# The last attention taken by pairs of heads, with four buffers and query tiles further ahead, and the shared keys and values prepared inside the fifth FFN

## The chip, the cores and the metric

The kernel runs on one core of a Trainium2 chip. The metric is the device time of one execution in microseconds. A profile of one execution shows what each engine did: PE (TensorE, with its weight loads as PEld), DVE (VectorE), ACT (ScalarE), POOL (GpSimd) and SP, which issues the weight transfers.

## What is computed

The reference is two blocks of two layers each on 256 tokens of width 1024, in float32. The first block has a convolution module, a sparse attention and two FFNs. The second puts 16 meta tokens ahead (272 positions) and has four FFNs, a gated linear attention, and last a sliding-window attention with sinks over keys and values that all its layers share. That last attention is what the change is about:

```python
def swa_mixer(hn, w_q, sinks, w_out, k, v, cos, sin):
    q = (hn @ w_q).reshape(B, L, N_KV_HEADS, GROUP, HEAD_DIM)      # 16 heads of 64, 4 to a key head
    q = apply_partial_rope(q, cos, sin) * (HEAD_DIM ** -0.5)
    ...
    # each block of 128 queries sees 16 meta keys, the block before and its own (masked)
    s = jnp.einsum('bkgnqd,bknsd->bkgnqs', q_blk, k_band)
    p = sink_softmax(s, mask, sink)          # exp(s-m) / (sum + exp(sink-m))
    o = jnp.einsum('bkgnqs,bknsd->bkgnqd', p, v_band)
    return o @ w_out
```

The keys and values come from `shared_kv`, a product of the stream after the fourth FFN with `w_kv`, with the keys rotated. They are thus known one FFN before the attention needs them.

## The kernel before

Activations lie transposed, 128 channels on the partitions and the tokens along the free axis, in eight tiles (KD = 8). Every weight tile of 128x1024 float32 comes by DMA into a ring of six slots; ACT makes its high part `wh` (L1704), DVE the low part `wl` (L1828, called through `ahead`), five tiles ahead of its use. A product is then three matmuls for each of eight k-steps (L1584): high by high, low by high, high by low, 24 for a tile of 256 columns.

The order of work on each engine is written out by hand; engines wait on counted semaphores. For unit u = 8 (the last attention) PE runs `swa_pe`, ACT `swa_act`, DVE `swa_dve`. PE first runs `begin`, an opening: it multiplies the first tiles by the high part of x as this arrives, then makes the mean of squares (L1635), from which ACT and DVE make the scale `rx` (L1766, L1845), then adds the low part (L1626). The opening takes two query tiles before; the third follows by itself.

A query tile holds two heads, h = 0 on partitions 0 to 63, h = 1 on 64 to 127. Its rotation is a matmul with `rot` on PE (`perm`, L1336) and three DVE operations (L1445 to L1447: sines, cosines, sum). The 16 heads are units n. For each, PE makes `scores(n)` (L1350, two matmuls of 144 and 272 columns over 64 rows), DVE adds the mask and finds the least (L1476), ACT makes the exponentials with their sums (L1418, L1420), DVE scales by the reciprocal (L1489 to L1492), PE turns the probabilities (`turned`: three large transposes L1361, two of the 16 meta keys L1363), ACT and DVE copy them out (L1429, L1506), PE multiplies by the values (`values`: L1376, L1377, L1379), and ACT and DVE split the result in high and low parts (`attn_hi` L810, `attn_lo` L814). Every one of these buffers is double. PE's loop over n has one query tile's matmuls on even n and one rotation on odd n, tile n // 2 + 3.

The keys' rotation (L1323 and L1445 to L1447) and the turning of the values (L1328, L1330, copies L1405, L1406) stand at the head of this unit. The fifth FFN (`ffn4_a`: 44 tiles, then `ffn4_b`) lies between the product that makes keys and values and this unit.

The earlier sparse attention (unit 2) already runs by pairs: `scores(p)` at L658 alternates two heads in different halves of the rows and different banks, `values(p)` at L695 and L697 two heads in different halves of the output columns, with buffers four deep.

## Time and profile before

| | |
|---|---|
| runs before | 1915.03 us median of 3 (1914.94 to 1917.54) |
| the profiled execution | 1917.76 us, its span 1916.0 us |
| mean granted TensorE clock | 0.957 of full speed |
| PE busy | 1839.4 us, 96% of the span |
| DVE busy | 1247.2 us, 65% |
| ACT busy | 917.1 us, 48% |

PE is busy nearly always by its record, but this is no limit in itself: matmuls are pipelined, and their records double when the granted clock is half. What a change is worth is read from its stretch of the trace: which engine the others wait for there, and at which clock PE ran.

### The profile page before, as it was taken

The numbers are of one execution on the slowest core, as the hardware profiler recorded it, in microseconds if no ns is written. First come the engines' busy times: TensorE is split into PE (matmuls) and PEld (weight loads), VectorE is DVE, ScalarE is ACT, GpSimd is POOL, SyncE is SP. The second block draws the span as 40 slices with busy tenths as digits, with TensorE's granted clock in tenths as the row PEclk, the third lists the DMA queues.
The fourth block names the chain that finished last, engine by engine and source line by source line (L and its number), as shares of the span: only waits on it lengthen the run. The fifth ranks groups of instructions, "written<-read, shape, count | busy, mean of one in ns | idle before, by whom it ended". The sixth has DMA issues, their size and how long they took to land.

```text
span 1916.0 us, 33032 instructions
## 1 busy us (share of the span) xinstructions
PE 1839.4 (96%) x13492; PEld 1711.9 (89%) x13492; DVE 1247.2 (65%) x2120; ACT 917.1 (48%) x1585; POOL 113.3 (6%) x150
## 2 busy tenths in 40 slices
PE   6989998999899999999999999999999998999997
PEld 6979997888479998999979879999999997589997
DVE  6867668774777666766564338665676657557764
ACT  7545443542755454544454235444554545445442
POOL 1001004300010001000100020000000000000000
PEclk9999999997899999999998979999999999789999
DMA  4214555541025555555533214555455551025553
GB/s 153 78 44 165 187 185 202 187 144 45 1 89 185 184 193 193 182 176 176 190 108 101 76 66 144 172 174 191 138 190 185 195 188 62 27 89 200 186 198 122
DMA packets 76038, 276.35 MB, mean 144 GB/s; under 512 B 8496, under 2 KB 9520, under 8 KB 75760
## 3 DMA queue, kind: packets, MB, share of 16 engines
q1 hardware_dynamic: 75168, 270.57, 42.1%
q8 instruction: 107, 1.75, 0.4%
q0 software_dynamic: 288, 2.30, 0.3%
q10 hardware_dynamic: 432, 1.38, 0.2%
q14 instruction: 43, 0.35, 0.1%
HBM read 273.16 MB, written 1.05 MB: 143 GB/s over the span
## 4 chain that ended last, share of the span: by engine, by line
PE 88%; DVE 7%; ACT 3%; DMA 1%; issue 1%; DVEq 0%; SPq 0%; ACTq 0%
PE acc L1584 43%; PE mix L1584 19%; PE acc L1580 4%; PE mix L265 3%; PE acc L1581 2%; PE acc L1604 2%; DVE wl L1828 2%; DMA arrived<-in_w 1%; PE acc L1089 1%; PE acc L1350 1%; PE stat L1635 1%; PE acc L1658 1%; PE acc L1092 1%; PE mix L1658 1%; PE mix L1604 1%
## 5 line engine op out<-in xcount | busy, mean ns | idle before, releaser
L1828 DVE TENSOR_TENSOR wl<-arrived,wh 128x1024 fp32r<-128x1024 f32 x514 | 641.6, 1249 | 400.1 <-ACT wh L1704 388.3
L1704 ACT ACTIVATE wh<-arrived 128x1024 fp32r<-128x1024 f32 x514 | 542.0, 1058 | 585.1 <-DMA arrived<-in_w 584.7
L1584 PE MATMUL acc<-xh,wh 128*128 128x256 f32 (+1 forms) x1512 | 432.6, 286 | 0.0
L1584 PE MATMUL acc<-xh,wl 128*128 128x256 f32 (+1 forms) x1512 | 430.4, 285 | 0.0
L1584 PE MATMUL acc<-xl,wh 128*128 128x256 f32 (+1 forms) x1512 | 430.2, 285 | 0.0
L1584 PE MATMUL acc<-hx,wh 128*128 128x256 f32 (+1 forms) x1664 | 304.3, 284 | 0.0
L1584 PEld LDWEIGHTS acc<-xh,wh 128*128 128x128 f32 x1512 | 287.1, 190 | 5.9 <-issue 5.2
L1584 PEld LDWEIGHTS acc<-xh,wl 128*128 128x128 f32 x1512 | 287.2, 190 | 0.0
L1584 PEld LDWEIGHTS acc<-xl,wh 128*128 128x128 f32 x1512 | 286.1, 189 | 0.2
L1584 PE MATMUL mix<-xh,wh 128*128 128x256 f32 (+1 forms) x968 | 278.8, 288 | 2.3 <-DVE y L1447 1.4
L1584 PE MATMUL mix<-xh,wl 128*128 128x256 f32 (+1 forms) x968 | 277.1, 286 | 0.0
L1584 PE MATMUL mix<-xl,wh 128*128 128x256 f32 (+1 forms) x968 | 276.7, 286 | 0.0
L1584 PEld LDWEIGHTS acc<-hx,wh 128*128 128x128 f32 x1664 | 258.9, 189 | 0.8 <-issue 0.8
L1584 PE MATMUL acc<-hx,wl 128*128 128x256 f32 (+1 forms) x832 | 236.6, 284 | 0.0
L1584 PEld LDWEIGHTS mix<-xh,wh 128*128 128x128 f32 x968 | 185.0, 191 | 5.0 <-DVE y L1447 1.9
L1584 PEld LDWEIGHTS mix<-xh,wl 128*128 128x128 f32 x968 | 185.0, 191 | 0.0
L1584 PEld LDWEIGHTS mix<-xl,wh 128*128 128x128 f32 x968 | 184.4, 191 | 0.2
L1584 PEld LDWEIGHTS acc<-hx,wl 128*128 128x128 f32 x832 | 157.0, 189 | 0.0
L1580 PE MATMUL acc<-hx,wh 128*128 128x512 f32 x416 | 149.1, 401 | 7.8 <-DVE wl L1828 6.8
L1581 PE MATMUL acc<-hx,wl 128*128 128x256 f32 x416 | 117.7, 283 | 0.0
L1580 PEld LDWEIGHTS acc<-hx,wh 128*128 128x128 f32 x416 | 79.3, 191 | 27.8 <-DVE wl L1828 8.0
L1546 POOL TENSOR_TENSOR sumsq<-sq 128x256 f32<-128x256 f32 (+1 forms) x11 | 11.8, 1076 | 1162.7 <-ACT sq L1779 777.0
(408 smaller groups left out, 2339.7 us busy)
## 6 DMA issues: line engine op xcount, KB each, us to landing
arrived<-in_w SPq DMA_DIRECT2D x514, 512.0 KB, 3.3
scr<-in_cmp_w POOLq DMA_DIRECT2D x1, 2048.0 KB, 8.9
x<-in_x ACTq DMA_DIRECT2D x2, 544.0 KB, 8.1
out<-x SPq DMA_DIRECT2D x8, 128.0 KB, 1.8
par<-in_par ACTq DMA_DIRECT2D x1, 259.0 KB, 4.5
scr<-in_positions POOLq DMA_DIRECT2D x1, 128.0 KB, 7.1
scr<-in_cmp_w POOLq DMA_DIRECT2D x1, 32.0 KB, 9.2
scr<-in_w_gate POOLq DMA_DIRECT2D x1, 32.0 KB, 2.9
```

The source lines that it names most:

```text
L265: ins = nc.tensor.matmul(mix[1 + j % 2][:, 0:SEQ], cdiag[:, j % 2, n, :], cu[:, j - 1, s:s + SEQ], start=(n == 0), stop=(n == PE_TAPS - 1))
L1089: ins = nc.tensor.matmul(dst, gv[base:base + w, n, 256 * h + P * v:256 * h + P * v + P], gatt[base:base + w, c % 2, h, 0:w], start=True, s ...
L1092: ins = nc.tensor.matmul(dst, gS[(c - 1) % 2][h][:, P * v:P * v + P], gq[:, h, s:s + w], start=False, stop=True)
L1350: ins = nc.tensor.matmul(acc[n % 2][:, c:c + e], sq_q[DH * h:DH * h + DH, j, q:q + P], sk[DH * h:DH * h + DH, j // 4, 0:e], start=True, st ...
L1580: nc.tensor.matmul(bank(name, t)[:, 0:2 * SEQ], wh[:, h.slot, w], hx[:, :, k, META:], start=(k == 0), stop=False)
L1581: ins = nc.tensor.matmul(bank(name, t)[:, 0:SEQ], wl[:, h.slot, w], hh[:, k, META:], start=False, stop=(k == kt - 1))
L1584: ins = nc.tensor.matmul(bank(name, t)[:, 0:L - c], w_part[:, h.slot, w], v_part[:, k, c:], start=(k == 0 and w_part is wh and v_part is h ...
L1604: nc.tensor.matmul(bank(name, t)[:, 0:L - c], w_part[:, slot, k * P:(k + 1) * P], hi[:, k, c:], start=(k == 0 and w_part is wh), stop=False)
L1635: ins = nc.tensor.matmul(stat[:, 0:L - c], ones[:], sq[:, k, c:], start=(k == 0), stop=(k == KD - 1))
L1658: ins = nc.tensor.matmul(bank(name, t)[:, 0:L - c], w_part[:, slot, w], v_part[:, k, c:], start=(k == 0 and w_part is wh and v_part is xh) ...
L1704: nc.scalar.activation(wh[:, h.slot, :], raw(h.slot), ACT.Copy).then_inc(w_hi, 1)
L1828: nc.vector.tensor_tensor(wl[:, h.slot, :], raw(h.slot), wh[:, h.slot, :].bitcast(F32), ALU.subtract).then_inc(w_lo, 1)
```

## The change

1. The keys' rotation and the turning of the values move into `ffn4_a`: after its tiles 0 to 3, 4 to 11, 12 to 19 and 20 to 27 PE runs one piece of `kv_turned` each, ACT copies after two of its double tiles (`kv_values`), DVE rotates after two (`kv_keys`). All use the bank `stat`. The second head's 16 meta values go to partitions 32 to 47, by an ordinary matmul with the identity and not a transpose.
2. The opening takes four query tiles instead of two, and the loop's query tile is p + 4.
3. The loop goes over eight pairs p of heads. Scores of a pair alternate heads (rows 0 to 63 and 64 to 127, banks `acc[0]` and `acc[1]`), values alternate heads in the halves of the output columns. Scores run two pairs ahead.
4. `sS`, `sP` and `sPT` have four buffers instead of two.
5. DVE scales a pair's probabilities with two tensor_tensor instead of four tensor_scalar, adds and inverts the sums of two heads at once, and copies the small transposes of a pair in one operation on 48 partitions.
6. The sines' part of a rotation is taken apart from the rest (`sines`, `rotated`), with its own semaphore; `attn_lo` runs two pairs behind.
7. ACT reads its exponential table ahead of the unit's first weight split.

```diff
-        sS = area(832).rearrange("p (b n) -> p b n", b=2)
-        sP = area(832).rearrange("p (b n) -> p b n", b=2)
-        sPT = area(768).rearrange("p (b n) -> p b n", b=2)
+        sS = area(1664).rearrange("p (b n) -> p b n", b=4)
+        sP = area(1664).rearrange("p (b n) -> p b n", b=4)
+        sPT = area(1536).rearrange("p (b n) -> p b n", b=4)
...
         def swa_pe(pe, gemm, begin, opening):
-            begin(8, ("swa_q", 0), ("swa_q", 1))
-            pe.wait_ge(s_kv, 4)
-            for m in range(2):
-                ins = nc.tensor.matmul(mix[1 + m][:, 0:L], rot[:], sk[:, m, :], start=True, stop=True)
-                ins.then_inc(s_perm, 1)
...
+            begin(8, ("swa_q", 0), ("swa_q", 1), ("swa_q", 2), ("swa_q", 3))
...
+            def scores(p):
+
+                pe.wait_ge(s_k, p + 1)
+                if p:
+                    pe.wait_ge(s_min, 2 * p)
+                for qt, (c, e, q) in enumerate(SQ):
+                    for h in range(2):
+                        ins = nc.tensor.matmul(acc[h][:, c:c + e], sq_q[DH * h:DH * h + DH, p, q:q + P], sk[DH * h:DH * h + DH, p // 4, 0:e],
+                                               start=True, stop=True)
+                        if qt:
+                            ins.then_inc(s_s, 1)
...
+            def values(p):
+
+                if p >= 2:
+                    pe.wait_ge(m_lo, 24 + p - 1)
+                for part in range(3):
+                    for h in range(2):
+                        n, g = 2 * p + h, 2 * (p // 4) + h
+                        w = slice(DH * g, DH * g + DH)
+                        dst = mix[p % 2][DH * h:DH * h + DH]
+                        if part == 0:
+                            pe.wait_ge(s_ptc, n + 1)
+                            nc.tensor.matmul(dst[:, 0:SEQ], sv[:, 0, w], sPT[:, n % 4, 0:SEQ], start=True, stop=False)
+                        elif part == 1:
+                            nc.tensor.matmul(dst[:, P:SEQ], sv[:, 1, w], sPT[:, n % 4, SEQ:SEQ + P], start=False, stop=False)
+                        else:
+                            pe.wait_ge(s_pmc, p + 1)
+                            r = slice(32 * h, 32 * h + META)
+                            nc.tensor.matmul(dst[:, 0:SEQ], sv[r, 2, w], sPM[r, p % 2, :], start=False, stop=True).then_inc(s_o, 1)
...
+            for p in range(KD + 1):
+                if p:
+                    values(p - 1)
+                if p + 2 < KD:
+                    scores(p + 2)
+                if p + 3 < KD:
+                    perm(p + 3)
+                if p < KD:
+                    turned(p)
+                if p + 4 < KD:
+                    pe.wait_ge(s_turn, p + 4)
+                    gemm("swa_q", xh, xl, META, None, first=p + 4, last=p + 5)
             gemm("swa_out", hh, hl, META, (m_lo, 24))
...
+            for p in range(KD):
+                t = p + 3
+                if 3 < t < KD:
                     query(t)
-                elif t < KD:
-                    rotated(2 + t, sq_q[:, t, :], SEQ, SEQ + META)
...
+                normal(p)
+                if t < KD:
+                    sines(t)
+                if p + 2 < KD:
+                    least(2 * p + 4)
+                    least(2 * p + 5)
+                if t < KD:
+                    rotated(t)
+                if p >= 2:
+                    attn_lo(dve, p - 2, 3)
+                dve.wait_ge(s_pm, p + 1)
+                if p >= 2:
+                    dve.wait_ge(s_o, 2 * p - 2)
+                nc.vector.tensor_copy(sPM[0:32 + META, p % 2, :], stat[0:32 + META, 0:SEQ]).then_inc(s_pmc, 1)
+                if t < KD:
                     ahead(BASE["swa_q"] + t)
...
-                    gemm("ffn4_a", xh, xl, cg(u), (x_lo, 8 * u))
+                    gemm("ffn4_a", xh, xl, cg(u), (x_lo, 8 * u), last=4)
+                    for i in range(4):
+                        kv_turned(pe, i)
+                        gemm("ffn4_a", xh, xl, cg(u), None, first=4 + 8 * i, last=12 + 8 * i)
+                    gemm("ffn4_a", xh, xl, cg(u), None, first=36)
```

On PE, what lay between two query tiles of the loop before (L1361 and L1363 turn one head, L1350 its scores, L1376 to L1379 its values, L1336 a rotation):

```order
L1361 MATMUL acc<-ident,scr 128x128 x3
L1363 MATMUL stat<-ident,scr 16x128 x2
L1350 MATMUL acc<-scr,y 128x144
L1350 MATMUL acc<-scr,y 128x272
L1376 MATMUL mix<-scr 64x256
L1377 MATMUL mix<-scr 64x128
L1379 MATMUL mix<-scr 64x256
L1336 MATMUL mix<-y,rot 128x256
L1361 MATMUL acc<-ident,scr 128x128 x3
L1363 MATMUL stat<-ident,scr 16x128 x2
```

and what lies there after the change (L1415 to L1421 values, L1379 scores, L1370 rotation, L1391 to L1401 the turning of a pair):

```order
L1415 MATMUL mix<-scr 64x256 x2
L1417 MATMUL mix<-scr 64x128 x2
L1421 MATMUL mix<-scr 64x256 x2
L1379 MATMUL acc<-scr,y 128x144 x2
L1379 MATMUL acc<-scr,y 128x272 x2
L1370 MATMUL mix<-y,rot 128x256
L1391 MATMUL acc<-ident,scr 128x128 x6
L1399 MATMUL stat<-ident,scr 16x128 x2
L1401 MATMUL stat<-ident,scr 16x128 x2
```

Two heads' work now stands as one block, each kind of matmul for both heads side by side, with the values of the pair before at its head (the rest of before's block, one head's scores and values, stands behind the second pair of rows there).

On DVE, the head of one pair's period before (the second head of a pair; L1489 to L1492 scaling, L1476 least, L1445 to L1447 rotation, L1828 a weight split):

```order
L1489 TENSOR_TENSOR scr<-scr 128x2
L1490 RECIPROCAL scr<-scr 128x2
L1492 TENSOR_SCALAR scr<-scr 128x144
L1492 TENSOR_SCALAR scr<-scr 128x272
L1476 ISA scr<-acc,scr 128x144
L1476 ISA scr 128x1
L1476 ISA scr<-acc,scr 128x272
L1476 ISA scr 128x1
L1445 TENSOR_TENSOR scr<-mix,sinT 128x256
L1446 TENSOR_TENSOR y<-y,cosT 128x256
L1447 TENSOR_TENSOR y<-y,scr 128x256
L814 TENSOR_TENSOR hx<-mix,hx 128x256
```

and the head of a period after (L1484 a query tile's evacuation, L1517 to L1521 the scaling of a pair, L1492 the sines, L1506 least):

```order
L1484 SCALAR_TENSOR_TENSOR y<-mix,rx 128x256
L1517 TENSOR_TENSOR scr<-scr 128x4
L1518 RECIPROCAL scr<-scr 128x4
L1521 TENSOR_TENSOR scr<-scr 128x2x144
L1521 TENSOR_TENSOR scr<-scr 128x2x272
L1492 TENSOR_TENSOR scr<-mix,sinT 128x256
L1506 ISA scr<-acc,scr 128x144
L1506 ISA scr 128x1
L1506 ISA scr<-acc,scr 128x272
L1506 ISA scr 128x1
L1506 ISA scr<-acc,scr 128x144
```

One scaling serves two heads, and the sines, for which PE waits before the next query tile, now stand ahead of the leasts.

## Rows read from the trace of the kernel before

**Rows 1.** The page's first line.

```profile
span 1916.0 us, 33032 instructions
```

**Rows 2.** Busy time by stretch: length, PE, PEld, DVE, ACT, POOL, granted clock, DMA share, GB/s.

```profile
1395.40:1506.00 110.60, 110.60 (x937) 110.60 (x936) 77.31 (x120) 53.91 (x79) 0.00 (x0) 1.00 0.56 186
...
1590.90:1602.40 11.50, 7.25 (x46) 5.50 (x45) 10.54 (x26) 6.40 (x11) 0.00 (x0) 0.94 0.37 129
1602.40:1607.90 5.50, 5.48 (x25) 5.48 (x26) 2.61 (x9) 1.20 (x5) 0.00 (x0) 0.50 0.00 0
1607.90:1644.90 37.00, 37.00 (x227) 26.12 (x226) 27.30 (x95) 17.89 (x55) 0.00 (x0) 1.00 0.17 58
...
1644.90:1652.40 7.50, 6.29 (x33) 3.50 (x31) 6.18 (x21) 3.62 (x11) 0.00 (x0) 0.99 0.22 70
1652.40:1683.20 30.80, 29.48 (x83) 14.68 (x83) 11.48 (x50) 9.63 (x34) 0.00 (x0) 0.50 0.00 1
1683.20:1707.50 24.30, 24.30 (x195) 24.30 (x195) 12.38 (x15) 11.87 (x17) 4.46 (x6) 0.93 0.45 152
```

**Rows 3.** Chain that ended last, one rotation and one head: start us, us, what.

```profile
1629.27 0.63 PE mix L1336 x2
1629.90 0.33 PE acc L1361 x3
1630.23 0.22 PE stat L1363 x2
1630.44 0.90 PE acc L1350 x4
1631.34 0.58 PE mix L1376 x2
1631.92 0.22 PE mix L1377 x2
1632.14 0.57 PE mix L1379 x2
```

**Rows 4.** The same chain, one head late in this attention, and `swa_out`.

```profile
1657.99 0.83 PE acc L1361 x3
1658.83 0.43 PE stat L1363 x2
...
1660.93 1.04 PE mix L1376 x2
...
1683.25 24.27 PE acc L1584 x192
```

**Rows 5.** Chain in the earlier attention: a pair's values begin, its scores follow.

```profile
509.26 0.57 PE mix L695 x2
...
510.70 0.86 PE acc L658 x8
```

**Rows 6.** Busy time by stretch, end of the earlier attention.

```profile
543.00:546.00 3.00, 2.12 (x18) 1.27 (x14) 1.91 (x7) 1.01 (x3) 0.00 (x0) 1.00 0.00 0
```

**Rows 7.** Timeline: first xh and `rx`, here and in the last FFN's opening.

```profile
1578.99 0.91 ACT L1717 ACTIVATE xh<-x,par 128x256 fp32r<-128x256 f32 x2 [2.95 <-DVE x L1861]
...
1589.08 1.75 DVE L1845 RECIPROCAL rx<-root 128x256 f32<-128x256 f32 x1 [1.12 <-ACT root L1766]
...
1712.52 0.91 ACT L1717 ACTIVATE xh<-x,par 128x256 fp32r<-128x256 f32 x2 [2.95 <-DVE x L1861]
...
1725.16 1.75 DVE L1845 RECIPROCAL rx<-root 128x256 f32<-128x256 f32 x1 [3.67 <-ACT root L1766]
```

**Rows 8.** Chain at the start of this attention: cosines of a rotation, one head's least.

```profile
1596.00 0.43 DVE y L1446
...
1600.32 0.79 DVE scr L1476 x4
```

**Rows 9.** Groups of instructions by form, 1590 to 1684: busy, mean ns, idle before.

```profile
L1828 DVE TENSOR_TENSOR wl<-arrived,wh 128x1024 fp32r<-128x1024 f32 x8 | 9.7, 1208 | 0.0
...
L1492 DVE TENSOR_SCALAR scr<-scr 128x272 f32<-128x272 f32 x16 | 5.7, 355 | 0.0
```

More of the change, by code:

```diff
@@ L1366, in values @@
[L1366 to L1379 removed]
+            pe.wait_ge(s_kk, 2)
@@ L1381, in swa_pe @@
             scores(0)
             perm(2)
-            for n in range(len(SUNITS) + 1):
-                if n + 1 < len(SUNITS):
-                    scores(n + 1)
-                if n:
-                    values(n - 1)
-                t = n // 2 + 3
-                if t < KD and n % 2 == 0:
-                    pe.wait_ge(s_k, t + 2)
-                    gemm("swa_q", xh, xl, META, None, first=t, last=t + 1)
-                elif t < KD:
-                    perm(t)
-                if n < len(SUNITS):
-                    turned(n)
+            scores(1)
@@ L1419, in exps @@
                                          accum_out=sstat[:, 8 + b + qt:9 + b + qt]).then_inc(s_exp, 1)
[L1420 removed]
+                nc.scalar.activation(sstat[:, 16 + b:18 + b], sstat[:, b:b + 2], ACT.Exp, bias=col("sinks", n)).then_inc(s_es, 1)
             exps(0)
[L1423 to L1433 removed]
@@ L1434, in swa_act @@
-            attn_hi(act, KD - 1, s_o, len(SUNITS))
+            exps(1)
+            for p in range(KD):
+                if p + 1 < KD:
+                    exps(2 * p + 2)
+                    exps(2 * p + 3)
+                for n in (2 * p, 2 * p + 1):
+                    act.wait_ge(s_pt, n + 1)
+                    if n >= 4:
+                        act.wait_ge(s_o, n - 3)
+                    nc.scalar.activation(sPT[:, n % 4, :], acc[2 + n % 2][:, 0:384], ACT.Copy).then_inc(s_ptc, 1)
+                if p + 3 < KD:
+                    ahead(BASE["swa_q"] + p + 3)
+                if p:
+                    attn_hi(act, p - 1, s_o, 2 * p)
@@ new lines, in normal @@
+            def normal(p):
+                b = 2 * (2 * p % 4)
+                dve.wait_ge(s_es, 2 * p + 2)
+                tot = sstat[:, 24 + b:28 + b]
+                if p >= 2:
+                    dve.wait_ge(s_p, p - 1)
+                step(nc.vector.tensor_tensor(tot, sstat[:, 8 + b:12 + b], sstat[:, 16 + b:20 + b], ALU.add))
+                step(nc.vector.reciprocal(tot, tot))
+                for qt, (c, e, q) in enumerate(SQ):
+                    v = sP[:, 2 * p % 4:2 * p % 4 + 2, c:c + e]
+                    ins = nc.vector.tensor_tensor(v, v, tot.rearrange("p (h q) -> p h q", h=2)[:, :, qt:qt + 1].to_broadcast([P, 2, e]), ALU.mult)
+                ins.then_inc(s_p, 1)
@@ L1465, in swa_dve @@
+            nc.vector.tensor_scalar(snk, par[:, COL["sinks"]:COL["sinks"] + 16], -1.0, None, ALU.mult).then_inc(s_nk, 1)
+            for t in range(3):
+                query(t)
+            sines(0)
+            rotated(0)
+            query(3)
+            sines(1)
+            rotated(1)
+            ahead(BASE["swa_q"])
             dve.wait_ge(s_nk, 1)
             dve.wait_ge(s_mask, 3)
-            def least(n):
-                j, h = SUNITS[n]
-                dve.wait_ge(s_s, n + 1)
-                if n >= 2:
-                    dve.wait_ge(s_es, n - 1)
-                b = 2 * (n % 2)
-                for qt, (c, e, q) in enumerate(SQ):
-                    ins = nc.vector.tensor_tensor_reduce(sS[:, n % 2, c:c + e], acc[n % 2][:, c:c + e], smask[:, c:c + e], 1.0,
-                                                         snk[:, 2 * j + h:2 * j + h + 1], ALU.add, ALU.min, sstat[:, b + qt:b + qt + 1])
-                ins.then_inc(s_min, 1)
@@ new lines, in swa_dve @@
+            least(0)
+            least(1)
+            sines(2)
+            rotated(2)
+            ahead(BASE["swa_q"] + 1)
+            least(2)
+            least(3)
+            ahead(BASE["swa_q"] + 2)
+            for p in range(KD):
+                t = p + 3
+                if 3 < t < KD:
+                    query(t)
+                normal(p)
[9 more added lines that the diff above has]
+                dve.wait_ge(s_pm, p + 1)
+                if p >= 2:
+                    dve.wait_ge(s_o, 2 * p - 2)
+                nc.vector.tensor_copy(sPM[0:32 + META, p % 2, :], stat[0:32 + META, 0:SEQ]).then_inc(s_pmc, 1)
+                if t < KD:
```

214 lines of the change are left out of this document (100 added, 114 removed).

## The prediction

> **What bounds the kernel now.** I read the page first, then the busy table by stretches, then the chain of waits through the last attention. The profiled span is 1916.0 us [rows 1]; its run took 1917.8 and the median is 1915.0, so a difference worked out on the span is applied to the median. The change touches the stretch from 1590.9, when the query norm is ready, to 1683.25, when `swa_out` begins, and a few instructions of `ffn4_a`. The reader should see four pieces in [rows 2]. In the first 11.5 us DVE is busy 10.54 us while PE mostly waits: DVE's queue is the bound. At its end the granted clock has left 2.4 GHz, and the 24 matmuls of query tile 3 take 5.5 us at 0.50. Then come four periods, one query tile and one pair of heads each, 37.0 us or 9.25 us a period, at full clock; PE is covered, DVE at 27.3 of 37.0. After the last query tile (1644.9) the clock holds for 7.5 us and then is 0.50 for the remaining 30.8 us, down to `swa_out`, whose first us still run slowly (24.3 us, mean clock 0.93).
>
> [rows 3] is the PE work of one head and of one rotation on the chain at full clock: rotation 0.63, three probability transposes 0.33, the two small ones 0.22, scores 0.90, values 0.58 + 0.22 + 0.57. Two heads and a rotation are 6.3 us; with about 2.95 of query matmuls that is the 9.25. PE is therefore the bound of the periods. At the low clock the same pieces double [rows 4]; `swa_out` then takes 24.27.
>
> **What a pair costs PE.** Before shows no paired score in this attention, but the earlier attention has them. There the four score matmuls of a pair (eight records; 128 and 256 columns, two heads on different halves of the rows) take 0.86 us [rows 5], for 384 columns a head; here 416 columns, so 0.92 instead of 1.80. The paired value matmuls there run from 509.26 to 510.70 [rows 5]: 1.44 us for two heads, against 2 x 0.80 here, so pairing side by side in columns saves little, 0.16. The third value matmul (16 rows of keys) has two heads on different rows and columns, which no row shows. Bounds: 0.57 if both run at once, 1.14 if one after the other. I take 0.75, nearer the scores, whose row halves overlap. Values: 2.2 for 2.74. Transposes: six large ones 0.66, two small 0.22, and the second head's two as ordinary matmuls, two 128-column matmuls of 0.22 [rows 3]: 1.35 for 1.10. A period is then 2.2 + 0.92 + 0.63 + 1.35 + 2.95 = 8.05 us.
>
> The Trainium skill (TensorEngine Tiling, Restrictions, Gotcha 1) says that different row tiles cannot access the same PSUM bank at once; both heads' third value matmul write one bank. By it the pair would take 1.14 there, a period 8.45, and the whole about 1.2 us more over three periods. No row here shows it.
>
> **The start.** Four query tiles in the opening instead of two put more ahead of the mean of squares. The opening of the last FFN has four tiles of the same shapes: from its first xh to its reciprocal 12.64 us, against 10.09 here [rows 7]. So rx comes 2.55 us later, at 1593.4. The two key rotations that DVE did after rx are gone from there (six operations of 272 columns, 0.45 each with their gaps, 2.7 us), so its first query again starts near 1593.5. Its queue until the first pair is normalised: three queries 1.7 (0.43 each and a hand-off to itself), rotation 0 1.35, query 3 0.5, rotation 1 1.35, a weight split 1.2, two heads' least 1.6, rotation 2 1.35, split 1.2, least 1.6, split 1.2, normalisation 1.5; with 0.4 for waits on PE 15.0 us, to 1608.4. The pieces are from [rows 8, 9]: 0.43 plus a small gap for each 256-column operation, 0.79 for a head's least, 1.21 for a split. The paired normalisation (two tensor_tensor over 288 and 544 columns) is bounded by what the two heads' four scalings take now, 0.355 for 272 columns and less for 144 [rows 9], about 1.2, and by 832 columns at 0.43 for 256, 1.4; I take 1.2, with the two small operations 1.5. PE idles through this much as before, so I expect the low clock at about the same place (the mean of 0.94 in the first piece puts the fall 1.4 us before its end, at 1601). Turning pair 0 at low clock is 2 x (0.83 + 0.43) [rows 4] plus 0.4: 2.95, to 1611.35. Query tile 4 starts slowly and gets its clock back within it, ending near 1615.5. Before it ended at 1617.2 (1607.9 plus one period): **-1.7**.
>
> **The periods.** DVE needs, a period: query 0.5, normalisation 1.5, rotation 1.35, least 1.6, low part 0.42, one copy of 256 columns 0.43 where two were, split 1.2: 7.0 us, below PE's 8.05; its wait for the rotation matmul lies inside that gap. So PE still bounds. Tiles 5, 6 and 7: 3 x (9.25 - 8.05) = **-3.6**, so that tile 7 ends at 1639.7.
>
> **The tail.** Call the end of tile 7 zero. PE does values 3, scores 6, rotation 7, transposes 4 to 5.1. DVE waits for rotation 7 until 3.9, then has sines 0.45, least 1.6, the rest of the rotation 0.9, low part, copy and split 2.05, so that it is free at 8.9; normalisation 5 ends at 10.4, and only then can PE turn pair 5. Meanwhile values 4 and scores 7 fit. From 10.4 on, at full clock, copy, normalisation and turning alternate: turned 5 to 11.75, copy 12.7, turned 6 to 15.6, values 6 to 17.9, turned 7 to 19.3, values 7 to 21.5. At low clock PE bounds: turning 2.95, values 4.05 (2 x (1.04 + 0.43), the 0.43 twice the 0.22 of [rows 3], less a tenth, plus 1.4), three times: 10.4 + 21.0 = 31.4.
>
> Which of the two is the question that decides most of the time. The clock fell at 1652 after a stretch in which PE's record is 6.29 us busy of 7.5 [rows 2], 1.2 us idle: one head at a time, half of the rows or columns. In the earlier attention pairs kept 1.00 at 2.12 busy of 3 us [rows 6]. The tail has pairs, but also a stretch (5.1 to 10.4) with about 3.1 us of 5.3 busy, and after that only values, 16-column products and transposes. I think it falls there. The Trainium skill (TensorE: Matmul & The Clock Gate, Part 4) says transposes do not count as busy for the clock in the same way; the fall at 1652 agrees, it only makes the fall likelier. So `swa_out` starts at 1639.7 + 31.4 = 1671.1 and not 1683.25, of which -5.3 are already counted: **-6.9** more. `swa_out` itself stays at 24.3.
>
> **In `ffn4_a`.** PE is busy 110.6 of 110.6 us over most of it [rows 2], so each inserted matmul is paid: four transposes 0.44, two small 0.22, two 128-column matmuls 0.44, two rotations of 272 columns 1.2 [rows 3]: **+2.3**. DVE's 2.7 us and ACT's 1.3 us more lie beside PE over several tiles; without that cover it would be 4 us. The waits there are for work finished at least four tiles before.
>
> Sum: -1.7 - 3.6 - 6.9 + 2.3 = **-9.9**, hence 1905.1 us.
>
> **Rivals.**
> The clock holds in the tail (pairs hold it in the earlier attention, [rows 6]). Tail 21.5, another 9.9 us off, and `swa_out` wholly fast, 1.6 off: 1893.6. 0.30.
> The pairs do not overlap here (they switch tile shapes more often than there). Values 2.74, scores 1.80: a period 9.4, the tail about 35 (its queue starts fuller than before's 38.35): -1.7 + 0.5 - 3.4 + 2.3 = -2.3: 1912.7. [rows 5] speaks against it. 0.08.
> Slower: the clock does not come back with tile 4. With half clock in the periods too, each costs 8 more, 24; the tail another 5, tile 4 two: about +31, so 1936. It decides once two of the three periods are at 0.50. Against it: 5.5 us of query matmuls brought it back at 1607.9, and the share of query matmuls in a period rises. 0.05.
> Hand-offs cost more than I count, 2 to 5 us over the stages: 1907 to 1910. 0.07.
>
> **The numbers.** The forecast 0.50, and the cases above. Differences under 0.2% (3.8 us) can't be told from none. Faster: 0.50 + 0.30 + most of the hand-offs = 0.87; within 0.2%: the case without overlap, 0.08; slower 0.05. The range for 8 in 10 takes in the case of the held clock and the dear hand-offs: 1891 to 1911. The forecast's own, with 0.57 to 1.14 for the third value matmul and 1 us each way at the start and in the periods: 1901 to 1909.
>
> **What would show it.** After: periods near 8.05 with PE covered; a pair's scores in 0.9; values 0, 1 and 2 of a pair in 1.44 and 0.57 to 1.14; the granted clock at 0.50 from about 1647 to `swa_out`; rx of the query norm 2.5 us later after its first xh; `ffn4_a` longer by 2.3. Wrong if the clock column reads 1.00 in the tail, or if DVE is covered in the periods and PE is not.

## The result: 1888.3 us, 1.4% faster, and why the forecast of 1905.1 was too high

The changed kernel takes 1888.3 us (median of 4 runs, 1886.2 to 1888.5) against 1915.0 us for the kernel before: ratio 0.9862, 95% interval 0.9844 to 0.9880. The direction was forecast rightly, the size was not: 26.7 us were gained where 9.9 were forecast, and 1888.3 lies below the range of 1891 to 1911.

The profiled executions differ by 29.9 us of span. The page's first line, which answers to [rows 1]:

```profile
span 1886.1 us, 32992 instructions
```

Busy time by stretch of the changed kernel: length, PE, PEld, DVE, ACT, POOL, granted clock, DMA share, GB/s. The stretches are cut where those of [rows 2] are: start, low clock, the periods, the tail, `swa_out`.

```profile
1590.90:1602.40 11.50, 7.81 (x56) 6.50 (x57) 8.79 (x23) 6.14 (x12) 0.00 (x0) 1.00 0.53 182
1602.40:1610.80 8.40, 5.69 (x31) 3.65 (x28) 7.75 (x26) 4.74 (x19) 0.00 (x0) 0.59 0.00 0
1610.80:1635.90 25.10, 25.10 (x201) 19.67 (x202) 20.40 (x60) 15.42 (x53) 0.00 (x0) 1.00 0.19 65
1635.90:1654.90 19.00, 15.82 (x127) 9.25 (x128) 14.28 (x47) 10.16 (x34) 0.00 (x0) 1.00 0.08 28
1654.90:1677.70 22.80, 22.80 (x194) 22.80 (x195) 12.39 (x15) 11.81 (x18) 4.46 (x6) 1.00 0.49 162
```

The reader is to see the clock column of the fourth line: 1.00 where [rows 2] have 0.50 for 30.8 us. The tail from the last query tile to `swa_out` lasts 19.0 us in place of 38.3, though PE is idle for 3.2 of them. The second thing is the third line: query tile 4 (3.04 us) and three periods of 7.35 us, not 8.05, with PE covered throughout.

The chain of waits of the changed kernel, one period, and below it the start of `swa_out` (start us, us, what). Values are L1415 to L1421, scores L1379, rotation L1370, turning L1391 to L1401, the query tile L1639; it answers to [rows 3] and the last of [rows 4]:

```profile
1613.85 0.58 PE mix L1415 x4
1614.44 0.22 PE mix L1417 x4
1614.66 0.58 PE mix L1421 x4
1615.23 0.90 PE acc L1379 x8
1616.14 0.63 PE mix L1370 x2
1616.77 0.66 PE acc L1391 x6
1617.42 0.22 PE stat L1399 x2
1617.64 0.54 PE stat L1401 x4
1618.18 3.03 PE mix L1639 x24
...
1654.85 22.80 PE acc L1639 x192
```

A pair of heads takes in each kind of product what one head took in [rows 3]: values 0.58 + 0.22 + 0.58, scores 0.90. The sum is 7.36.

What PE still waits for in the tail stands in its timeline (idle before, and who ended it, in brackets): once 1.65 us for the low part of an output, and for the scaling of pair 5 and the two after it 0.51, 0.35 and 0.54. All four are DVE's.

```profile
1641.86 0.65 PE L1415 MATMUL mix<-scr 128*64 128x256 f32 x4 [1.65 <-DVE hx L814]
...
1644.73 0.88 PE L1391 MATMUL acc<-ident,scr 128*128 128x128 f32 x6 [0.51 <-DVE scr L1521]
...
1648.28 0.87 PE L1391 MATMUL acc<-ident,scr 128*128 128x128 f32 x6 [0.35 <-DVE scr L1521]
...
1651.84 0.87 PE L1391 MATMUL acc<-ident,scr 128*128 128x128 f32 x6 [0.54 <-DVE scr L1521]
```

The first read of the stream by the query norm and `rx`, as in [rows 7]:

```profile
1580.12 0.91 ACT L1776 ACTIVATE xh<-x,par 128x256 fp32r<-128x256 f32 x2 [3.18 <-DVE x L1922]
...
1592.73 1.75 DVE L1906 RECIPROCAL rx<-root 128x256 f32<-128x256 f32 x1 [3.63 <-ACT root L1827]
```

They are 12.61 us apart, 2.52 more than in [rows 7] for this place; 2.55 was forecast.

### The profile page after: what moved, and what is told of

Its sections match the earlier page's. It is cut to its first block, busy times and chain, and to the rows that moved or that the text cites. A ratio compares the mean times of both kernels' runs of the same rounds, so it can differ in the third digit from the quotient of the medians.

```text
span 1886.1 us, 32992 instructions
## 1 busy us (share of the span) xinstructions
PE 1803.1 (96%) x13512; PEld 1692.3 (90%) x13512; DVE 1240.5 (66%) x2080; ACT 915.4 (49%) x1587; POOL 114.3 (6%) x150
## 3 DMA queue, kind: packets, MB, share of 16 engines
q10 hardware_dynamic: 432, 1.38, 0.2%
## 4 chain that ended last, share of the span: by engine, by line
PE 87%; DVE 7%; ACT 3%; DMA 2%; issue 1%; ACTq 0%; DVEq 0%
PE acc L1639 43%; PE mix L1639 19%; PE acc L1635 5%; PE mix L265 3%; PE acc L1636 2%; PE acc L1659 2%; DVE wl L1889 2%; DMA arrived<-in_w 1%; PE acc L1089 1%; PE mix L1659 1%; PE stat L1690 1%; PE acc L1092 1%; PE acc L1713 1%; PE mix L1713 1%; DVE xl L1901 1%
## 5 line engine op out<-in xcount | busy, mean ns | idle before, releaser
L1639 PE MATMUL acc<-xh,wh 128*128 128x256 f32 (+1 forms) x1504 | 429.8, 286 | 0.0
L1639 PE MATMUL acc<-xh,wl 128*128 128x256 f32 (+1 forms) x1504 | 427.4, 284 | 0.0
L1639 PE MATMUL acc<-xl,wh 128*128 128x256 f32 (+1 forms) x1504 | 427.1, 284 | 0.0
L1639 PE MATMUL acc<-hx,wh 128*128 128x256 f32 (+1 forms) x1664 | 302.9, 283 | 0.0
L1639 PEld LDWEIGHTS acc<-xh,wh 128*128 128x128 f32 x1504 | 284.8, 189 | 5.3 <-issue 4.7
L1639 PEld LDWEIGHTS acc<-xh,wl 128*128 128x128 f32 x1504 | 284.9, 189 | 0.0
L1639 PEld LDWEIGHTS acc<-xl,wh 128*128 128x128 f32 x1504 | 283.7, 189 | 0.2
L1639 PE MATMUL mix<-xh,wh 128*128 128x256 f32 (+1 forms) x960 | 275.9, 287 | 0.9 <-DVE wl L1889 0.9
L1639 PE MATMUL mix<-xh,wl 128*128 128x256 f32 (+1 forms) x960 | 274.5, 286 | 0.0
L1639 PE MATMUL mix<-xl,wh 128*128 128x256 f32 (+1 forms) x960 | 274.2, 286 | 0.0
L1639 PEld LDWEIGHTS acc<-hx,wh 128*128 128x128 f32 x1664 | 257.6, 188 | 0.4 <-issue 0.4
L1639 PE MATMUL acc<-hx,wl 128*128 128x256 f32 (+1 forms) x832 | 236.0, 284 | 0.0
L1639 PEld LDWEIGHTS mix<-xh,wh 128*128 128x128 f32 x960 | 183.0, 191 | 2.4 <-DVE wl L1889 1.1
L1639 PEld LDWEIGHTS mix<-xh,wl 128*128 128x128 f32 x960 | 183.1, 191 | 0.0
L1639 PEld LDWEIGHTS mix<-xl,wh 128*128 128x128 f32 x960 | 182.3, 190 | 0.1
L1635 PE MATMUL acc<-hx,wh 128*128 128x512 f32 x416 | 148.3, 400 | 10.2 <-DVE wl L1889 9.2
L1639 PEld LDWEIGHTS acc<-hx,wl 128*128 128x128 f32 x832 | 156.3, 188 | 0.0
L1635 PEld LDWEIGHTS acc<-hx,wh 128*128 128x128 f32 x416 | 78.9, 190 | 30.1 <-DVE wl L1889 10.5
L1636 PEld LDWEIGHTS acc<-hx,wl 128*128 128x128 f32 x416 | 79.3, 191 | 0.0
```

What stands on the lines that cost most here:

```text
L1635: nc.tensor.matmul(bank(name, t)[:, 0:2 * SEQ], wh[:, h.slot, w], hx[:, :, k, META:], start=(k == 0), stop=False)
L1636: ins = nc.tensor.matmul(bank(name, t)[:, 0:SEQ], wl[:, h.slot, w], hh[:, k, META:], start=False, stop=(k == kt - 1))
L1639: ins = nc.tensor.matmul(bank(name, t)[:, 0:L - c], w_part[:, h.slot, w], v_part[:, k, c:], start=(k == 0 and w_part is wh and v_part is h ...
```

## How the experiments are compared

The work ahead of this attention varies by some microseconds from one execution to the next: the first xh comes between 1575.6 and 1581.9 in kernels that barely differ before it. So each trace is measured from its own first xh, in four pieces that end where query tile 4, query tile 7, the tail and `swa_out` end. The sum is worked out from these cuts of each chain; the time is the median of the runs (one run where no interval stands), the ratio that to the kernel before on the same chip.

| kernel | to tile 4 | 3 periods | tail | `swa_out` | sum | time | ratio to before, 95% |
|---|---|---|---|---|---|---|---|
| before | 38.2 | 27.7 | 38.3 | 24.3 | 128.5 | 1915.0 | |
| changed | 33.7 | 22.0 | 19.0 | 22.8 | 97.5 | 1888.3 | 0.9844 to 0.9880 |
| e1, heads serial | 33.7 | 26.2 | 24.4 | 22.8 | 107.1 | 1897.2 | 0.9871 to 0.9939 |
| e2, values serial | 33.7 | 26.2 | 24.4 | 22.8 | 107.0 | 1896.8 | |
| e3, before, 6 dummies | 38.3 | 27.8 | 27.0 | 24.7 | 117.9 | 1904.7 | 0.9922 to 0.9965 |
| e4, before, 24 dummies | 38.4 | 27.7 | 30.1 | 22.6 | 118.9 | 1906.4 | |
| e5, opening of two | 35.8 | 22.0 | 19.0 | 22.8 | 99.6 | 1888.4 | 0.9845 to 0.9910 |
| e6, keys late | 42.6 | 22.0 | 19.0 | 22.8 | 106.4 | 1895.8 | 0.9881 to 0.9941 |
| e7, two buffers | 34.5 | 29.4 | 37.6 | 22.8 | 124.3 | 1913.8 | 0.9985 to 1.0023 |
| e8, splits later | 32.2 | 22.0 | 18.6 | 22.8 | 95.6 | 1888.6 | 0.9837 to 0.9909 |
| e9, e8 and dummies at the start | 29.9 | 22.0 | 18.6 | 22.8 | 93.3 | 1885.5 | 0.9825 to 0.9860 |
| e10, dummies at the start | 32.8 | 22.0 | 19.0 | 22.8 | 96.6 | 1886.9 | 0.9823 to 0.9861 |
| e11, e7 and dummies in the tail | 33.7 | 28.3 | 33.2 | 22.8 | 118.1 | 1909.6 | |
| e12, a longer wait in the tail | 33.8 | 22.0 | 23.2 | 22.8 | 101.8 | 1890.4 | 0.9852 to 0.9896 |

The theory formed from the two traces was that the gain is made of three parts: a clock that no longer falls in the tail, products of two heads that overlap wholly, and deeper buffers that let both happen. The rivals were that it is the overlap alone, or that the head of the stage gave it.

## Experiments on the overlap: e1 and e2

In e1 the heads of a pair are issued one after the other, in scores and values; in e2 in the values alone.

```diff
-                for qt, (c, e, q) in enumerate(SQ):
-                    for h in range(2):
+                for h in range(2):
+                    for qt, (c, e, q) in enumerate(SQ):
...
-                for part in range(3):
-                    for h in range(2):
+                for h in range(2):
+                    for part in range(3):
```

Expected of e1:

> The changed kernel, but the two heads of a pair one after the other in scores and in values. Theory 1 (side by side, two heads' matmuls overlap on PE, and that both saves PE time and keeps the clock up): scores of a pair 1.8 us and values 2.74 instead of 0.90 and 1.38, a period of 9.4 instead of 7.35, and the clock falls in the tail, which takes 30 to 35 us instead of 19: about 1908 to 1912. Theory 2 (the overlap saves PE time, the clock is kept by something else, such as fewer or shorter idle stretches): same periods, but clock 1.00 in the tail, 23 to 26 us: about 1900.

Expected of e2:

> The changed kernel with only the values one head after the other. If the column halves overlap (as the 1.38 us for two heads says): values 2.74 a pair, a period 8.7, over three periods +4 us, the tail +3 at full clock, so 1894 to 1897; with the clock lost in the tail 1903 to 1908. If the column halves had nothing to do with the 1.38: values stay at 1.4 and the time at 1888.

The chain of waits of e1, values and scores of a period:

```profile
1612.90 0.58 PE mix L1415 x2
1613.48 0.22 PE mix L1417 x2
1613.70 0.57 PE mix L1421 x2
1614.27 0.58 PE mix L1415 x2
1614.84 0.22 PE mix L1417 x2
1615.06 0.57 PE mix L1421 x2
1615.63 0.91 PE acc L1379 x8
```

The values take 2.74 us for a pair in place of 1.38, so alternating the heads halves them; eight pairs lie after tile 4, three in the periods and five in the tail, where part of it falls into waits for DVE: 3 x 1.38 and 5.4, 9.5 in the sum, 8.9 in the medians. The scores take 0.91 in e1 as they do alternated. Two heads on different halves of the rows overlap in whichever order they are issued, and [rows 3] have 0.90 for one head alone. So e1 and e2 are the same kernel as far as time goes. The granted clock is 1.00 in the whole tail of both: the overlap of the values is not what keeps it. Of e1's expectations, the second had the clock and the tail (24.4 in its 23 to 26) but not the periods, which it left as they were; the first had the values right and the scores and the clock wrong. e2 came out as its first case at full clock said (a period of 8.7, 1896.8 in 1894 to 1897), with one run and a tail 5.4 longer where it had 3.

## Experiments on the clock: e3, e4 and e12

e3 is the kernel before with six 128-column matmuls, whose result is not used, ahead of the turning of head 10, in the wait in which its clock fell. e4 adds three more ahead of each of the six later passes, the last of them after the last turning, 24 in all.

```diff
+                if n == 10:
+                    pe.wait_ge(s_k, 10)
+                    for _ in range(6):
+                        nc.tensor.matmul(mix[2][:, 0:P], ones[:], ident[:], start=True, stop=True)
                 if n < len(SUNITS):
                     turned(n)
```

Expected of e3:

> The kernel before with six extra small matmuls (their result unused, 1.35 us) in the idle stretch of PE ahead of the eleventh head, where the granted clock fell. Theory idle (the gap there lost the clock): the tail runs at full clock, 38.35 us become about 22, and swa_out 1.5 less: 1897 to 1900. Theory load (one head at a time loads the array too little to hold the clock): it falls all the same a few us later, at most 3 us gained: 1911 to 1915.

Expected of e4:

> As the run with six extra matmuls, and three more (0.7 us) for each later head, 3.5 us of added PE work. Theory idle: 1 to 4 us slower than with six alone. Theory load: if six alone do not hold the clock, these may, and then the time is 1898 to 1903 where six alone leave 1911 to 1915.

Busy time by stretch of e3, one microsecond each, about where its clock does fall:

```profile
1667.00:1668.00 1.00, 1.00 (x7) 0.46 (x5) 0.00 (x0) 0.00 (x0) 0.00 (x0) 1.00 0.00 0
1668.00:1669.00 1.00, 0.42 (x3) 0.29 (x2) 0.41 (x1) 0.49 (x1) 0.00 (x0) 0.85 0.00 0
1669.00:1670.00 1.00, 1.00 (x4) 0.46 (x2) 0.00 (x0) 0.00 (x0) 0.00 (x0) 0.50 0.00 0
```

It falls at 1668.7, some 16 us later than before, and the tail is 27.0 us in place of 38.3 with before's own work and all its waits in it. Some 1.6 us of useless work bought 11.1 us of time (1904.7 against 1915.8 of before on the same chip). In e4 the clock reads 1.00 to the end and `swa_out` is wholly fast, but the dummies themselves are on the path: tail 30.1. So the clock alone is worth 11 us here at least: the last 2.6 us of e3's tail and the first 4.2 of its `swa_out` still ran at 0.50. The rest of the gain in the tail, 27.0 to 19.0, came with the changed kernel's order and buffers. Neither of e3's theories had this: one expected the clock to hold to the end (1897 to 1900), the other a fall a few us later (1911 to 1915), and it fell 16 us later, in a wait of 0.58. Two of e3's nine runs took 1897.1 and 1898.4, with a mean clock of 0.970 and 0.969 where the others had 0.964 to 0.966; no trace of them shows where the clock stood. e4 is 1.7 us slower than e3 in its one run, as its first theory had it (1 to 4).

e12 asks from the other side how much room the changed kernel has. Four more additions on DVE make PE's longest wait of the tail longer.

```diff
+                if p == 4:
+                    dve.wait_ge(s_k, KD)
+                    for _ in range(4):
+                        step(nc.vector.tensor_tensor(snt[:, 0:SEQ], cosT[:, 0:SEQ], sinT[:, 0:SEQ], ALU.add))
                 if p >= 2:
                     attn_lo(dve, p - 2, 3)
```

> The changed kernel with four more additions of 256 columns on VectorE (about 0.4 us each, 1.7 us; their result is not used) ahead of the low part of pair 2's output, for which TensorE waits 1.65 us after the last query tile. It makes that wait 3.3 us in the changed kernel's tail, the longest there, and asks how much room the clock has. Theory one, the length of a wait decides: the clock falls during it, as it did in waits of 2.7 and 4.5 us, and with some 12 us of TensorE's work of the tail still to come at half clock the tail takes about 30 us in place of 19 and swa_out starts slowly: time 1899 to 1903. Theory two, the clock holds through one such wait: the tail is 1.7 us longer and the time 1889 to 1891.

The timeline of e12, the end of that wait, and its busy time by stretch: the wait, the work behind it, and the two microseconds in which the clock falls and comes back.

```profile
1639.38 0.76 PE L1415 MATMUL mix<-scr 128*64 128x256 f32 x4 [3.61 <-DVE hx L814]
```

```profile
1635.10:1639.40 4.30, 0.69 (x8) 0.33 (x6) 4.09 (x15) 3.87 (x14) 0.00 (x0) 1.00 0.00 0
1639.40:1646.10 6.70, 6.70 (x34) 3.67 (x34) 4.57 (x15) 1.26 (x3) 0.00 (x0) 0.53 0.00 0
...
1639.00:1640.00 1.00, 0.62 (x6) 0.42 (x8) 1.00 (x3) 0.00 (x0) 0.00 (x0) 0.90 0.00 0
...
1646.00:1647.00 1.00, 1.00 (x9) 0.61 (x8) 0.73 (x4) 0.72 (x3) 0.00 (x0) 0.69 0.00 0
```

Neither theory has what happened. The clock does fall, as theory one has it, but not in the wait: it reads 1.00 through all 3.61 us and falls at 1639.8 (a microsecond that starts at 1.00 and ends at 0.50 with a mean of 0.90 has its fall 0.8 in), when PE has been at work again for 0.4 us. And it does not stay low: 6.8 us later, at 1646.6, it is back, with no query tile in between. The tail costs 4.2 us more, of which 1.96 are the wait itself (3.61 for 1.65), and not the 11 that theory one priced. The time, 1890.4, lies in the 1889 to 1891 of theory two, whose clock was to hold: that is luck. It moved by 2.1, less than the intervals tell apart.

The length of the wait in which the clock falls thus tells little. At the start of the changed kernel, PE's timeline and two of the microseconds there:

```profile
1602.11 0.97 PE L1379 MATMUL acc<-scr,y 64*128 64x144 f32 x8 [2.72 <-DVE scr L1506]
1605.79 1.76 PE L1379 MATMUL acc<-scr,y 64*128 64x144 f32 x8 [2.71 <-DVE scr L1506]
```

```profile
1602.00:1603.00 1.00, 0.89 (x8) 0.57 (x8) 0.96 (x3) 1.00 (x6) 0.00 (x0) 1.00 0.00 0
1603.00:1604.00 1.00, 0.08 (x2) 0.00 (x0) 1.00 (x2) 0.58 (x3) 0.00 (x0) 0.59 0.00 0
```

The clock stood through the first wait, of 2.72 us, and through the scores behind it, and fell at 1603.2, 0.1 us into the second. The sharpest case is e7 and e11 (below), which are the same program up to the values of the fifth pair. Each has the same wait ahead of the turning of pair 1:

```profile
1619.30 1.54 PE L1391 MATMUL acc<-ident,scr 128*128 128x128 f32 x6 [0.93 <-DVE scr L1521]
```

```profile
1619.49 0.88 PE L1391 MATMUL acc<-ident,scr 128*128 128x128 f32 x6 [0.94 <-DVE scr L1528]
```

e7 (the first) lost the clock in it, at 1619.0, and its six transposes took 1.54 us; e11 (the second) kept it. So whether one wait loses the clock is not fixed by its length, nor by the work of the program around it alone.

The same stretch in the kernel before is different:

```profile
1652.50:1675.00 22.50, 22.50 (x64) 11.69 (x65) 9.42 (x42) 8.37 (x31) 0.00 (x0) 0.50 0.00 0
```

PE had work without a break for 22.5 us, one head at a time, and the clock never rose in it; it had fallen at 1652.3 and was low for 34.1 us. So a fall was a lasting one before. After the change it need not be, though pair work alone is no warrant of it. In e7 (below) the clock was low from 1653.2 to 1680.5, with two more waits for DVE or ACT in that time, and 7.1 us of the same kinds of matmuls without a break left it low:

```profile
1655.50:1662.60 7.10, 7.10 (x32) 3.84 (x32) 2.72 (x6) 0.00 (x0) 0.00 (x0) 0.50 0.00 0
```

That is no contradiction to e12, where PE had worked for 7.2 us when the clock rose, but more than at the changed kernel's start, where it rose after 4.2 (1605.79 to 1610.0).

## Experiments on the buffers: e7 and e11

e7 is the changed kernel with `sS`, `sP` and `sPT` two deep and the waits to match. e11 is e7 with twelve dummy matmuls ahead of the values of each pair from the fifth pair on.

```diff
-                if n >= 4:
-                    act.wait_ge(s_pt, n - 3)
-                    act.wait_ge(s_pm, n // 2 - 1)
-                b = 2 * (n % 4)
+                if n >= 2:
+                    act.wait_ge(s_pt, n - 1)
+                    act.wait_ge(s_pm, n // 2)
+                b = 2 * (n % 4)
...
-                    if n >= 4:
-                        act.wait_ge(s_o, n - 3)
+                    if n >= 2:
+                        act.wait_ge(s_o, n - 1)
```

Expected of e7:

> The changed kernel with two buffers for sS, sP and sPT, not four. Theory depth (four buffers let DVE, ACT and PE work on different pairs): exponentials of the next pair wait for the turning of this one, then least and scaling wait, each period 2 to 3 us longer: 1898 to 1908, and the clock may fall in the tail. Theory overlap (pairs on PE are the gain): PE stays the bound of the periods at 7.35 us, and only the tail grows by 1 to 3 us: 1889 to 1892.

Expected of e11:

> The changed kernel with two buffers in place of four and twelve dummy matmuls ahead of the values of each pair from the fifth on, inside TensorE's waits of 3 to 4.5 us there. It divides the loss of the run with two buffers (some 25 us) into waits and clock. Theory: some 18 us of TensorE's busy time in that run's tail was at half clock, so with the clock kept the tail is 7 to 9 us shorter and swa_out as long as before; the remaining 16 to 18 us are waits for ScalarE and VectorE: time 1904 to 1908. Rival one: the clock is all of it, 1890. Rival two: the clock is none of it, since the waits end when ScalarE and VectorE do: 1912 to 1915.

PE's timeline in the tail of e7, where its longest wait ends:

```profile
1650.34 0.61 PE L1401 MATMUL stat<-ident,scr 128*16 128x128 f32 x4
1655.47 1.12 PE L1415 MATMUL mix<-scr 128*64 128x256 f32 x4 [4.53 <-DVE hx L814]
```

The waits of e7, all engines, from 1640 to 1682 (engine line <- who ended it: us in total, times, longest us):

```profile
ACT scr L1457 <- PE stat L1401: 24.2, 4, 7.4
DVE scr L1506 <- ACT scr L1459: 12.3, 6, 5.8
...
PE mix L1415 <- DVE hx L814: 9.8, 3, 4.5
```

With two buffers the exponentials of a pair (L1457) wait until the pair before has been turned, DVE waits for the exponentials, and PE for DVE. Nothing of a pair runs ahead, and a pair needs both buffers at once. The whole gain is gone: 1913.8, ratio 0.9985 to 1.0023. Theory depth had the mechanism and the period (9.8 us for 7.35, where it expected 2 to 3 more), and missed the time (1898 to 1908), since the tail grew by 18.6 us and not only the periods. In e11 the clock reads 1.00 throughout the tail, which is then 33.2 us instead of 37.6: 4.3 less, where the theory had 7 to 9. Its one time, 1909.6, lies between the theory (1904 to 1908) and the second rival (1912 to 1915): part of the waits end when ScalarE and VectorE do, whatever the clock, and twice the dummies run up to the values with no wait left, so that they cost something themselves. The sum is 6.2 shorter, the time 4.2 in one run. Only 4.3 of the 6.2 are the dummies' doing: the other 1.9 lie ahead of the first of them, where e7's clock was low for 10.2 us at the start (e11: 6.8) and for another 3.4 from 1619.0. So of the 26.7 us that two buffers cost in the sum, some 20 are waits and some 6 are clock.

## Experiments on the start: e5, e6, e8, e9 and e10

e5 opens with two query tiles and runs tiles 2 and 3 behind it. e6 puts the keys and values back at the head of this unit. e8 moves DVE's weight splits out of the start of the attention.

```diff
-            begin(8, ("swa_q", 0), ("swa_q", 1), ("swa_q", 2), ("swa_q", 3))
+            begin(8, ("swa_q", 0), ("swa_q", 1))
+            gemm("swa_q", xh, xl, META, None, first=2, last=4)
```

> The changed kernel with two query tiles in the opening and tiles 2 and 3 after it, as plain products. If the four-tile opening is what shortened the start: rx comes 2.5 us earlier, but tiles 2 and 3 (5.7 us of PE) end at about the same point, and DVE's third query waits for them 1 to 2 us; so within 2 us of the changed kernel, 1887 to 1890. If the opening hides much of the norm's latency: 3 to 5 us slower, 1891 to 1893.

> The changed kernel with the keys' rotation and the turning of the values back at the head of the last attention. ffn4_a gets back 2.2 us. The head of the attention is bound by DVE, which gets 2.7 us of rotations and waits for PE and ACT between them, some 2 us more: net +2 to +4, so 1890 to 1892. Rival: PE's 2.2 us are worth as much as DVE's, and the time stays at 1888.

```diff
-            rotated(1)
-            ahead(BASE["swa_q"])
+            rotated(1)
...
-            ahead(BASE["swa_q"] + 1)
             least(2)
             least(3)
-            ahead(BASE["swa_q"] + 2)
...
-                if t < KD:
-                    ahead(BASE["swa_q"] + t)
+                if p < 4:
+                    ahead(BASE["swa_q"] + p)
...
+            for m in range(4, KD):
+                ahead(BASE["swa_q"] + m)
```

> The changed kernel with DVE's weight splits of the attention later: three out of its queue at the start (3.6 us), one a period in the first four, the last four after the loop, beside swa_out. If DVE's queue is what bounds the start and the tail: start 3 to 3.6 us shorter, tail 1.1 shorter, 1883 to 1885, about 1 us less still if the low clock in the start is shorter. If PE's or ACT's chain is close behind: under 2 us. Risk: swa_out's tiles 1 to 3 wait for their low parts, +1 to +3.

e5 lengthens the start by 2.1 us and the time not measurably, within its first case; its clock was low there for 10.2 us and not 6.8. e6 lengthens it by 8.9 us and gives back the 2.2 in `ffn4_a`; its time is 7.5 us above the changed kernel's, so moving this work under the FFN is worth a quarter of the whole gain, and the rest of the stage is the same to 0.1 us. Its forecast of 2 to 4 us missed: it counted DVE's work and waits, and in the trace the clock is also low for 17.1 us there (1600.8 to 1617.9) and not for 6.8. e8 shortens the stage by 1.9 in its trace, 1.5 at the start and 0.4 in the tail, and not by the 4 that its first case had; "under 2 us", for another chain close behind, is what came. Its median shows none of it; the trace's first xh comes 1.8 later, at 1581.88.

In e8 the clock still falls before the third scores. e9 adds eight dummy matmuls in each of PE's two waits there, e10 adds twelve in each to the changed kernel.

```diff
             scores(0)
             perm(2)
+            pe.wait_ge(s_q, 4)
+            turn8(8)
             scores(1)
+            turn8(8)
```

> The changed kernel with the weight splits of VectorE moved later, and eight dummy matmuls (their result is not used) in each of TensorE's two waits ahead of the second and the third scores. Theory: the start of the attention pays for a clock that fell in those two waits; at full clock the third scores, the rotation and the first turning take 2.95 us in place of 5.59 as they did in the run with the splits moved alone, so query tile 4 ends some 2.6 us sooner after the first read of the norm (29.6 us in place of 32.2), the rest is unchanged, the span is near 1883 and the time 1884 to 1887. Rival: VectorE alone sets the start, and the turning waits for it at full clock: no more than 1 us shorter.

> The changed kernel with twelve dummy matmuls in each of the two waits ahead of the second and third scores, nothing else moved. Theory: as before, 2.3 to 2.9 us off the start (31 us from the norm's first read to query tile 4's end in place of 33.7), time 1885 to 1887. Rival: nothing, because VectorE's queue (splits of 0.27 and 1.14 us) is what is late, 33.7 us.

The chain of waits of e9 from the third scores on:

```profile
1604.52 0.90 PE acc L1379 x8
1605.42 0.63 PE mix L1370 x2
1606.05 0.66 PE acc L1391 x6
1606.71 0.22 PE stat L1399 x2
1606.92 0.54 PE stat L1401 x4
1607.46 3.04 PE mix L1645 x24
```

From the third scores to query tile 4 it is 2.94 us where the low clock made it 5.03 in the changed kernel (1605.79 to 1610.82). e9's start is 29.9 us, which its theory gave as 29.6. It has the lowest median of all, 1885.5 (1884.5 to 1889.6). Its interval overlaps the changed kernel's, so that it beats the kernel before is shown, and that it beats the changed kernel is only likely: the stage is 4.2 us shorter in the trace, the medians 2.8. e10's rival was nearer: with the splits still in DVE's queue the start is 0.9 shorter, not 2.3 to 2.9, because the turning then waits for the scaling. That its 1886.9 lies in the theory's 1885 to 1887 is luck; it is not told apart from 1888.3.

## Why the prediction was wrong, step by step

**What held.** `ffn4_a`: the inserted work shifted its end by 2.23 us (the product that began at 1506.12 begins at 1506.85, while at the FFN's start, 1389.4, the changed trace was 1.50 ahead), forecast 2.3. The opening: `rx` 2.52 later, forecast 2.55. PE bounds the periods. The scores, 0.90, forecast 0.92. By luck: the first pair was scaled at 1608.2, forecast 1608.4, but the first xh came 1.1 later than before, so that the queue was 28.1 us long from there and not 29.4.

**The step that failed** is "I think it falls there", on the clock in the tail. It held. The prediction priced the other case as a rival at 0.30, with a tail of 21.5; the tail measured 19.0. Of the 38.3 us of before, e3 gives 11.3 to the clock alone. The argument counted PE's idle time, and set the 1.2 us idle of 7.5 in [rows 2] beside 3.1 idle of 5.3 that it expected. The changed kernel did idle so (3.2 of 19.0, once 1.65 at a stretch) and kept the clock, while before lost it in a wait of 1.28. Idle time by itself thus did not tell the two apart. It was no accident of one trace: the tail reads 1.00 in the traces of e1, e2, e5, e6, e8, e9 and e10 too, which have the same four buffers and the same wait of 1.65. Nor was it the overlap of the values, since e1 kept the clock without it. What differs besides is that before issued scores and transposes for one head at a time, and the other kernels for two. The price of a fall was wrong as well: the forecast had the low clock last from the fall to `swa_out`, as before, 9.9 us dearer, and where e12 made it fall it was back after 6.8 us and cost 2.2 beyond the longer wait.

**The term that was mis-sized** is "Values: 2.2 for 2.74". It measured 1.38. The 1.44 us taken from [rows 5] as the time of a pair's values in the earlier attention was in part the first head's product running alone, while the second's input was awaited. The timeline of before there, PE and ACT:

```profile
509.19 1.08 PE L695 MATMUL mix<-scr 128*64 128x256 f32 x3
509.85 0.43 PE L697 MATMUL mix<-scr 128*64 128x128 f32 x2
510.11 0.38 PE L695 MATMUL mix<-scr 128*64 128x256 f32 x1
...
509.30 0.49 ACT L793 ACTIVATE scr<-stat 128x384 f32<-128x384 f32 x1 [0.29 <-PE stat L673]
```

ACT copies the second head's probabilities until 509.79, and PE's values for that head can't begin before. The chain shows such a wait as no piece of its own when the head before fills it, and the five pairs that it shows from 509 on take 1.44 to 1.46 each. From this the prediction drew that halves of the columns "save little". They overlap wholly, given that both heads' inputs are there and that the heads are issued in turn (e1). The third value matmul, 16 rows, took 0.58 for both heads; the bounds were 0.57 and 1.14, and 0.75 was taken. The Trainium skill (TensorEngine Tiling, Restrictions, Gotcha 1) has different row tiles unable to access one PSUM bank at the same time. Here they lie on rows 0 to 15 and 32 to 47 and write one bank, in different halves of its partitions, and the trace shows no cost (0.58 for both, 0.57 for one in e1): the measurement does not bear the page out here.

**The sum again**, on the spans: start -4.5 (forecast -1.7), periods -5.7 (-3.6), tail -19.3 (-6.9), `swa_out` -1.5 (0), `ffn4_a` +2.2 (+2.3), and -1.1 by which the rest of the trace differs (1.5 ahead at the FFN's start, 0.4 more at its end, where the last weights came late): -29.9. The tail holds 12.4 us of the error of 20. Some 10 of those are the clock, by the forecast's own two cases (31.4 and 21.5). Of the other 2.5 the values of pairs 3 and 7 are 0.8 each, and 0.6 is DVE's queue between rotation 7 and the scaling of pair 5, 5.9 us (1638.8 to 1644.7) where 6.5 were forecast; the rest is under 0.2 apiece. The start's error is mostly the clock too: it was back at 1610, before query tile 4, so this took 3.04 and not 4.2, and the turning 2.12 and not 2.95. The periods' error is three times 0.7, the values' 0.82 less 0.07 more in the turning and 0.08 in the query tile.

**Where the gain comes from.** Counted in the stage's sum, 31.0 us: the clock that stays up 10.7 (e3); the overlap of the values 9.5 (e1); the remaining 10.8, between e3 and e1, is 4.6 in the start, from which work was moved, 1.6 in the periods (scores 0.9 less a pair, turning 0.3 more), 2.6 in the tail, and 1.9 in `swa_out`, which in e3 still begins at low clock. Part of these 10.8 is thus clock again, the 1.9 and some 1.3 of the 2.6 us that e3's tail still spent at 0.50. With two buffers nearly none of the gain is left (e7).

**What stays open.** Why the clock of the kernel before fell in its tail when the changed kernel's stood. The two waits, 1.28 and 1.65 us, don't explain it, and e7 and e11 show that a wait of the same length, in the same place of the same program, can go either way. That one head's work occupies half of the array is the difference that the traces offer, and the long low stretch of before fits it, but e3 kept 1.00 for 16 us of that same work, and no run held everything else equal. Nor is it settled why the order of issue matters for the values and not for the scores. The paired scaling, the sines taken apart and ACT's early table read had no run of their own; what they give is somewhere in the 10.8.

## What to carry to other kernels

Before taking the duration of a group of paired instructions from a chain, look in the timeline whether the second one's input was there; where it was not, the row gives a wait and no price. A stretch at low clock is priced twice, once for what falls and once for whether the work that follows brings it back, and six dummy matmuls in the wait where the clock falls find out cheaply what it is worth (11 us here). The length of a single wait does not say whether the clock will fall in it. Deeper buffers and a new order are one change: with the order alone the gain was nil, since a pair takes up both of two buffers.

## What the runs showed of the hardware

- Two heads' value products on different halves of the output columns: 1.38 us for a pair issued in turn, 2.74 issued one head after the other.
- Two heads' score products on different halves of the rows: 0.90 in turn, 0.91 one head after the other, and 0.90 for a single head.
- The granted clock stood through waits of 2.72 us (changed kernel, start) and 1.65 (its tail). It fell within waits of 1.28 (before), 0.58 (e3), 0.93 (e7, where e11 kept it through 0.94) and 4.53 (e7), and behind one of 3.61 when PE had been at work for 0.4 us (e12).
- The low stretch lasted 6.8 us at the start of the kernel before (1601.1 to 1607.9) and of the changed one, and in e12's tail; 10.2 at the start of e5 and e7, 17.1 at that of e6, 27.3 in e7's tail and 34.1 in the tail of before, 22.5 of them single-head work without a break.
